# A 12-stage float32 network on one core: the sparse-attention stage rewritten

## The reference

```
hn = rms_norm(h); p = hn @ o_w_in          # q(512) kc vc ks vs kw vw (128 each) gl(24) bg cg hd (512 each)
k_cmp, v_cmp = compress(kc), compress(vc)  # 15 windows of 32 tokens: gelu((window + pos) @ w1) @ w2
o_c = masked_softmax(q . k_cmp / 8) @ v_cmp
o_s = masked_softmax(rope(q) . rope(ks) / 8, causal) @ vs
o_w = masked_softmax(rope(q) . rope(kw) / 8, causal window) @ vw
yc  = gate0 * o_c + gate1 * o_s + gate2 * o_w          # gates = sigmoid(gl), per head and token
yd  = bg * causal_conv3(cg * hd)
h   = h + concat(yc, yd) @ o_w_out
h   = h + moe(rms_norm(h))
```

## Time and profile before

| | us |
|---|---|
| median of 3 runs | 2113.72 |
| the runs | 2109.43, 2113.72, 2114.61 |
| the profiled execution | 2109.94 |
| its span | 2107.9 |
| granted TensorE clock, mean | 0.989 |

### The profile page before, as it was taken

One profiled execution on the slowest core, in us unless ns is written; L12 is line 12 of the kernel. 1 busy time (PEld: TensorE's weight loads), 2 busy tenths in 40 slices (PEclk: granted clock), 3 DMA queues, 4 the chain that ended last, 5 costly groups with the idle time before them and its releaser, 6 DMA issues.

```text
span 2107.9 us, 31941 instructions
## 1 busy us (share of the span) xinstructions
PE 2016.6 (96%) x11820; PEld 1767.6 (84%) x11820; DVE 1577.1 (75%) x2176; ACT 1150.0 (55%) x1687; POOL 394.0 (19%) x192
## 2 busy tenths in 40 slices
PE   7999999999999999999999999999987999999997
PEld 6888987888888889888889998888975888888885
DVE  6777886677777769677778666777785588888887
ACT  5445543554454455554455535445445577777775
POOL 2222003232222310122322432223000300000000
PEclk9999999999999999999999999999998999999999
DMA  8555520455645554355544005555451588888895
GB/s 341 186 194 169 179 90 15 169 197 187 196 167 197 180 187 152 120 179 195 184 170 150 2 15 182 185 194 192 160 180 39 180 331 327 325 327 325 325 329 190
DMA packets 73395, 401.22 MB, mean 190 GB/s; under 512 B 8256, under 2 KB 8384, under 8 KB 41152
## 3 DMA queue, kind: packets, MB, share of 16 engines
q1 hardware_dynamic: 72848, 398.07, 54.1%
q10 hardware_dynamic: 432, 1.57, 0.2%
HBM read 398.57 MB, written 1.05 MB: 190 GB/s over the span
## 4 chain that ended last, share of the span: by engine, by line
PE 76%; DVE 13%; PEld 4%; ACT 3%; issue 2%; POOL 0%; DMA 0%; SPq 0%; ACTq 0%; PEldq 0%; DVEq 0%; POOLq 0%
PE psum L744 18%; PE psum L306 13%; PE psum L307 13%; PE psum L308 13%; PE psum L748 9%; DVE w_lo L290 4%; PE psum L969 2%; PE psum L957 2%; ACT w_hi L283 1%; PE psum L2803 1%; DVE w_lo L296 1%; PE psum L320 1%; PEld psum L306 1%; PEld psum L308 1%; PEld psum L307 1%
## 5 line engine op out<-in xcount | busy, mean ns | idle before, releaser
L290 DVE TENSOR_TENSOR w_lo<-ring,w_hi 128x1024 fp32r<-128x1024 f32 x498 | 742.7, 1521 | 179.4 <-ACT w_hi L283 178.0
L283 ACT ACTIVATE w_hi<-ring 128x1024 fp32r<-128x1024 f32 x744 | 739.9, 1051 | 234.2 <-PEq L500 129.1
L296 POOL TENSOR_TENSOR w_lo<-ring,w_hi 128x1024 fp32r<-128x1024 f32 x132 | 324.0, 2455 | 1079.7 <-ACT w_hi L283 1079.7
L744 PE MATMUL psum<-fT,w_hi 128*128 128x512 f32 x1760 | 422.4, 391 | 12.9 <-DVE w_lo L290 10.5
L744 PEld LDWEIGHTS psum<-fT,w_hi 128*128 128x128 f32 x1760 | 329.6, 188 | 84.3 <-issue 7.6
L306 PE MATMUL psum<-w_hi,hT_hi 128*128 128x384 f32 (+4 forms) x896 | 321.7, 359 | 12.4 <-POOL w_lo L296 4.0
L308 PE MATMUL psum<-w_hi,hT_lo 128*128 128x384 f32 (+4 forms) x896 | 310.7, 347 | 0.0
L307 PE MATMUL psum<-w_lo,hT_hi 128*128 128x384 f32 (+4 forms) x896 | 310.3, 346 | 0.0
L306 PE MATMUL psum<-w_hi,act_hi 128*128 128x512 f32 x616 | 242.4, 394 | 5.5 <-DVE act_lo L842 4.6
L307 PE MATMUL psum<-w_lo,act_hi 128*128 128x512 f32 x616 | 241.2, 392 | 0.0
L308 PE MATMUL psum<-w_hi,act_lo 128*128 128x512 f32 x616 | 239.9, 390 | 0.0
(11 more groups left out here) (485 smaller groups left out, 2413.9 us busy)
## 6 DMA issues: line engine op xcount, KB each, us to landing
ring<-in_stream SPq DMA_DIRECT2D x249, 1024.0 KB, 5.4
ring<-in_stream SPq DMA_DIRECT2D x248, 512.0 KB, 4.3
tables<-in_tables SPq DMA_DIRECT2D x1, 2261.0 KB, 19.9
gain_row<-in_gains ACTq DMA_DIRECT2D x3, 512.0 KB, 3.7
rows<-in_rows SPq DMA_DIRECT2D x1, 1288.0 KB, 22.6
X<-in_x SPq DMA_DIRECT2D x1, 1024.0 KB, 5.0
result<-X SPq DMA_DIRECT2D x2, 512.0 KB, 3.3
columns<-in_columns SPq DMA_DIRECT2D x1, 993.0 KB, 15.0
```

Of the source, the lines that this page charges most:

```text
L283: act.activation(part(w_hi, g, i), ring[:, k, i * PART:(i + 1) * PART], ACT.Copy) \
L290: dve.tensor_tensor(part(w_lo, g, i), ring[:, k, i * PART:(i + 1) * PART], part(w_hi, g, i).bitcast(F32), ALU.subtract) \
L296: pool.tensor_tensor(part(w_lo, g, 2), ring[:, k, 2 * PART:STEP], part(w_hi, g, 2).bitcast(F32), ALU.subtract) \
L744: pe.matmul(psum[:, 4 + 2 * (s % 2) + o, :], w[0][:, o, k, :], fT[:, k, :, :].rearrange("p a c -> p (a c)"), start=k == 0, stop=False, ski ...
```

## The change

The sparse stage keeps its operations but for these:

- The mask is added by PE: `scores_tensor(masked=True)` issues a third matmul with a bf16 identity and a bf16 view of the mask. The maxima are reduced straight from PSUM, and ACT's exps read PSUM with the scale (`masked_max_vector`, `masked_exp_scalar`); a score bank is then marked used by the exps.
- The columns of cg, hd and bg come in another order. cg is multiplied by the square of the row, and hd's copy multiplies by cg, so that the separate product is gone. The row copy stands at step 1.
- The rotations, the windows, the transposes of the rotated q and keys and the scores of group 0 move in among the projections; its maxima and exps too. The transposes of n_tok stand after step 4, the scores after step 5.
- DVE splits the last parts of the compression steps and of the output's first step; POOL does none of them. The output's first step is split before the attention's later groups.
- Products go group by group into both banks of o; the compressed branch comes last.
- The output's first step begins with its convolution half (k = 4 to 7), ahead of and between the transposes of o.
- No `keep_warm` is left in the stage.
- Buffers: half of n_S lies over one parity of w_hi and w_lo; n_zb, n_rope, the squared row and group 0's exps lie in O; other small tiles share space.

```diff
-        def scores_tensor(pe, stage, label, q, k):
+        def scores_tensor(pe, stage, label, q, k, masked=False):
             b = open_bank(pe, label)
-            pe.matmul(b[:, 0:P], q[:, 0:P], k[:, 0:P], start=True, stop=True)
-            pe.matmul(b[:, P:UNIT], q[:, P:SEQ], k, start=True, stop=True).then_inc(*stage.tensor(label))
+            pe.matmul(b[:, 0:P], q[:, 0:P], k[:, 0:P], start=True, stop=not masked, skip_group_check=masked)
+            ins = pe.matmul(b[:, P:UNIT], q[:, P:SEQ], k, start=not masked, stop=not masked, skip_group_check=masked)
+            if masked:
+                ins = pe.matmul(b[:, 0:UNIT].rearrange("p (b c) -> p b c", c=P)[:, 0::2, :], ident_bf16, bias_bf16[:, 0::2, :],
+                                start=False, stop=True, skip_group_check=True)
+            ins.then_inc(*stage.tensor(label))
...
+        def masked_max_vector(dve, stage, name, units, scale, small):
+            for i, u in enumerate(units):
+                dve.wait_ge(*after(f"{u}"))
+                dve.tensor_reduce(small[:, i, :], bank(u)[:, 0:UNIT].rearrange("p (b c) -> p b c", c=P), AX.X, ALU.max).then_inc(*stage.vector())
...
+        def masked_exp_scalar(act, stage, name, units, S, scale, less, sums):
+            act.wait_ge(*after(f"{name} max"))
+            for i, u in enumerate(units):
+                for t, cols in enumerate((slice(0, P), slice(P, UNIT))):
+                    act.activation(S[:, i, cols], bank(u)[:, cols], ACT.Exp, scale=scale, bias=less[:, i, t:t + 1], accum_out=sums[:, i, t:t + 1]) \
+                       .then_inc(*stage.scalar(f"{name} exp"))
+                marks[f"used {u}"] = marks[f"{name} exp"]
...
 PE, sparse_tensor
-            proj_tensor(pe, "sparse", g0, N_KINDS, at, between={2: turn_plain})
+            proj_tensor(pe, "sparse", g0, N_KINDS, at, between={2: turn_plain, 4: turn_rotated, 5: lambda: scores(0)})
-                        keep_warm(pe, b, 0 if which else 11)
+            scores(1)
...
+            turn_units(0)
...
+            scores(2)
...
+            turn_units(1)
+            scores(3)
+            turn_units(2)
...
+            for i in range(3):
+                products(i)
+            turn_units(3)
+            products(3, (0,))
+            finish(0)
+            products(3, (1,))
+            finish(1)
...
+            conv_part(0)
+            turn_tensor(pe, "sparse", sparse, 4, [f"used sparse o {t}" for t in range(TT)], ts=(0,))
+            conv_part(1)
+            turn_tensor(pe, "sparse", sparse, 4, [f"used sparse o {t}" for t in range(TT)], ts=(1,))
+            out_tensor(pe, "sparse", at, 4, begun=((0, 0), (0, 1)))
...
 ACT, sparse_scalar
+            proj_copies_scalar(act, "sparse", at, N_KINDS, n_place, {2: plain}, ahead=True,
+                               later={4: gate, 5: rotated, 7: lambda: exps(0)})
...
+            hidden(0)
+            split_hi(act, c0 + SPARSE_C, c0 + SPARSE_C)
+            hidden(1)
...
+            exps(1)
...
+            turned_units(0)
+            exps(2)
...
+            turned_units(1)
+            exps(3)
+            turned_units(2)
...
+            out_scalar(act, at, "sparse", "used sparse o 1", sparse, 4, ahead=1, turned=turned)
...
 DVE, sparse_vector
+            proj_copies_vector(dve, "sparse", at, N_KINDS, n_place, ahead=True, lasts=range(len(N_KINDS)), row_at=1, scale_of=n_scale,
+                               later={3: lambda: (squared_row(), rotate(0)), 4: lambda: rotate(1), 5: windows, 6: lambda: largest(0)})
+            split_lo(dve, c0 + 1, c0 + 1)
+            split_lo_last(dve, c0 + 1, c0 + 1)
+            weights(0)
+            split_lo(dve, c0 + 2, c0 + 2)
+            split_lo_last(dve, c0 + 2, c0 + 2)
+            tap(0)
+            split_lo(dve, c0 + 3, c0 + 3)
+            split_lo_last(dve, c0 + 3, c0 + 3)
+            largest(1)
...
+            tap(1)
+            weights(1)
+            largest(2)
...
+            tap(2)
+            weights(2)
+            largest(3)
...
+            weights(3)
+            does("sparse conv", dve.tensor_tensor, hT_lo[:, 4:8, :], n_conv[:, :, :], hT_hi[:, 4:8, :].bitcast(F32), ALU.subtract)
+            turn_vector(dve, "sparse", sparse, 4)
+            out_vector(dve, "sparse", at)
...
 POOL
-            split_lo_last(pool, g0, g0)
```

More of the change, by code:

```diff
@@ L524, in proj_tensor @@
                     wait_split(pe, g)
-                for k in range(KT):
+                ks = range(tiles if (s, j) in begun else KT)
+                for k in ks:
                     if isinstance(source, int):
@@ new lines, in scores, with turn_units @@
+            def scores(i):
+                pe.wait_ge(*after("used sparse kt 1"))
+                for u in range(4 * i, 4 * i + 4):
+                    s = u % SLOTS8
+                    scores_tensor(pe, sparse, f"sparse s {u}", n_qr[slot_rows(s), s // 2, :], n_kt[slot_rows(s), u // SLOTS8, :], masked=True)
+            def turn_units(i):
+                for u in range(4 * i, 4 * i + 4):
+                    turn_unit_tensor(pe, sparse, f"sparse pt {u}", n_exps(i)[:, u % 4, :], f"sparse p {i}")
@@ new lines, in products @@
+            def products(i, ts=range(TT)):
+                for u in range(4 * i, 4 * i + 4):
+                    pe.wait_ge(*after(f"used sparse pt {u}"))
+                    br, s = divmod(u, SLOTS8)
+                    for t in ts:
+                        for j, pt in enumerate(unit_blocks(n_unit(u), t)):
+                            v = (VS, VW)[br] + 64 * (s % 2)
+                            pe.matmul(bank(f"sparse o {t}")[:, 64 * s:64 * s + 64], pt, n_tok[:, j, v:v + 64], start=u == 0 and j == 0, stop=False,
+                                      skip_group_check=True)
@@ L1683, in sparse_tensor, with finish @@
+            def finish(t):
+                pe.wait_ge(*after("used sparse vcmp"))
+                pe.wait_ge(*after(f"used sparse pct {t}"))
+                pe.matmul(bank(f"sparse o {t}"), n_pct[:, t, :], n_vcmp.rearrange("p s d -> p (s d)"), start=False, stop=True,
+                          skip_group_check=True).then_inc(*sparse.tensor(f"sparse o {t}"))
+            proj_tensor(pe, "sparse", g0, N_KINDS, at, between={2: turn_plain, 4: turn_rotated, 5: lambda: scores(0)})
             for s in range(SPARSE_C):
@@ L1699, in sparse_tensor @@
                 release(pe, "sparse c", s)
[L1700 to L1706, removed]
-                for i, c0 in enumerate((KS, KW)):
-                    ins = pe.transpose(b[:, i * P:(i + 1) * P], n_tok[:, t, c0:c0 + P], ident)
-                ins.then_inc(*sparse.tensor(f"sparse kt {t}"))
+            scores(1)
             for which in range(2):
@@ L1715, in sparse_tensor @@
                 ins.then_inc(*sparse.tensor(f"sparse hid turned {which}"))
-            pe.wait_ge(*after("used sparse kt 1"))
-            def scores(units):
-                for u in units:
-                    s = u % SLOTS8
-                    scores_tensor(pe, sparse, f"sparse s {u}", n_qr[slot_rows(s), s // 2, :], n_kt[slot_rows(s), u // SLOTS8, :])
-            scores(range(0, 4))
+            turn_units(0)
             pe.wait_ge(*after("used sparse hid turned 1"))
@@ L1788, in sparse_scalar @@
                 split_hi(act, g, g)
[L1789 to L1799 removed]
+            hidden(0)
+            split_hi(act, c0 + SPARSE_C, c0 + SPARSE_C)
+            hidden(1)
+            act.activation(warm[:, :], eps, ACT.Exp)
             for which in range(2):
@@ L1851, in windows @@
                 wait_proj(dve, "sparse", N_KINDS, range(SPARSE_K, SPARSE_K + 2))
-                settle()
+                for which in range(2):
+                    does(None, dve.memset, n_zb[which][:, :, :, CMP_N:], 0.0)
                 for which, pos in enumerate(("pos_k", "pos_v")):
```

240 lines of the change are left out of this document (137 added, 103 removed).

## The result

| | before | after |
|---|---|---|
| median (14 runs each) | 2113.24 us | 2118.85 us |
| range | 2108.14 to 2114.61 | 2113.55 to 2123.64 |
| profiled execution, span | 2109.94, 2107.9 | 2117.55, 2115.6 |

The ratio is 1.0029, 95% interval 1.0021 to 1.0037: 5.6 us slower, where 2102.2 was forecast. In the two traces the sparse stage, from its first projection matmul to the first expert matmul (PE line L2803 before, L2932 after), takes 187.08 us before (1478.18 to 1665.26) and 192.78 after (1480.20 to 1672.98). The 2.0 us by which it starts later in the profile after were lost far ahead of it; subtract them when comparing places. Each kernel has one trace, and its execution need not be a typical one: that of before lies 3.3 us under its median, that of after 1.3.

The account below looks back on a forecast made before the run. DVE was taken to bound 1563 to 1602 us, a serial PE tail 1602 to 1639. Step 1 12.2 us earlier, less 2.5, saves 9.7: forecast 2102.2 us, own range 2099 to 2106, eight in ten 2095 to 2109.

Parts of the forecast that it names:

- the signs by which the prediction said it would be wrong: Compression's first matmul after 1557, output step 1 before 1622 or after 1632, or expert stage length changed by over 2 us.
- the first product: After exps 3 end, near 1597, the first product matmul was to run at clock 0.50.
- no idle before the first channel-major tile: In the projections, moving the row copy to step 1 frees the bank: PE's 2.94 us wait at 1508.36 goes.
- the wait in step 7: In the projections, tile (7, 1) waits for unit 0's exps to free its bank: 1.8 us lost on PE.
- the four PSUM reductions: In attention on DVE, a group's maxima become four reductions straight from PSUM, taking 1.9 us.
- products to step 1: Convolution half, transposes, then ACT's and POOL's work: output step 1 can start 13.2 us after the products.
- the expert stage: Behind the sparse stage, PE-bound: its length stays within 2 us, and a shift passes through to the kernel's end.
- I take 0.13, the nearer row: Score groups on PE: each added mask matmul costs 0.13 us, at most 0.4, so 2.2 us for a group.
- The products themselves pay: 5 us at half clock lose 2.5 us: Products after exps 3: fillers gone, PE's clock starts at half and recovers after 5 us, losing 2.5 us.
- the sum: Start of output step 1: 12.2 us earlier, less 2.5 for half clock in step 1, gives 9.7 us saved.
- the fourth: Products never lift the clock; products, convolution and transposes run at half: 8.8 us slower, 2121 us; chance 0.06.
- Rival 2: More half clock, from the 2.7 us gap before compression, or costlier masks and maxima: saves 4 to 7 us; chance 0.15.

Follow-up runs that it names:

- z1: The changed kernel with only the four mask matmuls of each group issued ahead of its score matmuls, no fillers: 2109.93 us, ratio 0.9985.
- x4: The changed kernel with 51 filler matmuls added ahead of compression, two groups' transposes, the products and output step 1: 2106.22 us, ratio 0.9979.
- y1: x4 with each group's four mask matmuls issued together ahead of its score matmuls: 2101.24 us, ratio 0.9952 against the kernel before.
- z4: y1 with group 0 masked on VectorE and without the 11 fillers ahead of compression: 2096.20 us, ratio 0.9924 against the kernel before.
- x1: The changed kernel with twelve filler matmuls ahead of the first product: 2113.63 us, ratio 1.0009 against the kernel before.
- x3: The kernel before without its 12 fillers ahead of the third group's transposes and 16 ahead of the output: 2112.66 us, ratio 1.0004.

## Why the prediction was wrong

Places in us from the stage's start. "Part 2 ends" is the end of the second token tile's products; the last row is the stage's length.

| | before | forecast | after | z1 | x4 | y1 | z4 |
|---|---|---|---|---|---|---|---|
| compression starts | 76.6 | 76.6 | 80.0 | 76.7 | 80.6 | 80.6 | 74.5 |
| exps 3 end | 123.1 | 118.5 | 128.3 | 119.4 | 123.7 | 120.0 | 115.4 |
| part 2 ends | 145.0 | 135.2 | 149.1 | 142.4 | 142.3 | 138.7 | 134.0 |
| step 1 starts | 160.6 | 148.4 | 162.0 | 155.3 | 155.2 | 151.5 | 146.9 |
| expert matmuls | 187.1 | 177.4 | 192.8 | 186.6 | 183.4 | 178.3 | 175.0 |

Of the signs by which the prediction said it would be wrong, two came. In times of the trace of before, the first compression matmul comes at 1558.2 (80.0 into the stage; the limit was 1557) and step 1 starts at 1640.2 (162.0; the limit was 1632). And the first product, which was to come at clock 0.50, came at 1.00.

Right, by the same steps: no idle before the first channel-major tile; the wait in step 7, 1.8 reckoned, 1.77 found; the four PSUM reductions, 1.9 reckoned and 1.94 found (1.87 in the chain); products to step 1, 13.2 reckoned, 162.0 - 149.1 = 12.9 found, with 3.68 us of idling for 3.7 and a loss of 7.08 - 4.4 = 2.7 in step 1 for 2.5; the expert stage, 442.6 us in both. With both causes mostly gone (y1) the stage takes 178.3 us against the forecast's 177.4; part of that agreement is luck, since step 1 is still 3.1 us late there and the way from it to the expert matmuls 2.2 us shorter than reckoned, without the lost clock in step 1 that the forecast had.

**The step that failed first: "I take 0.13, the nearer row ... the upper end adds 1 us here and 1 us to each later group".** Both ends were prices of the added instruction, 0.13 and 0.4. The cost was in its neighbours: 0.69 a unit, 0.38 of it the overlap of the two units around it. The hint was there: the four units of the earlier trace rows are on row halves in turn and take at most 0.44 us each, and I read that as the price of one unit and not as half that of a pair. Group 0 took 4.1 us for 2.2. Then the clock fell behind the wait in step 7, from 1549 to 1552, for a loss of 1.7 us. So compression started 3.4 us late. Grouping the masks undoes it: 8.9 us alone, 5.0 beside fillers.

**The step that failed second: "The products themselves pay: 5 us at half clock lose 2.5 us".** The clock was at 1.00 when they began, so the gaps ahead of them, which I had counted as the fall, had not lowered it yet; it fell 1.8 us into them and came back only at 1624, in the transposes behind them. The 72 products took 13.93 us for 8.1, 5.8 lost, and the transposes 0.7 more, where the sum had 2.5. And the sum had no half clock for the groups before them, since I counted only idle gaps as causes. The clock fell at about 1576 and 1587 while PE was busy with scores and masks, and the compressed scores took 6.13 us for 3.25. From compression's start to the end of exps 3 the chain needed 48.3 us for 41.9; 43.2 in x4, 39.5 in y1. So there the clock was worth 5.2 us and the parted pairs 3.7, more together than the 6.4 that were lost: the rest of the chain is 2.4 us shorter than I reckoned.

Of the 5.7 us + 9.7 us between forecast and stage (15.4), then: 3.4 by the start of compression, 6.4 from there to exps 3, 4.1 in the products, 0.3 less on the way to step 1, and 1.8 behind it, of which 1.6 in the fillers ahead of the expert matmuls, at half clock after (4.7 us for 14, before 3.1). That last fall was in no term of the sum either. The single removals are worth 12.6 (x4) and 8.9 us (z1), both together 17.6 (y1): they overlap by 3.9. In part that is because a parted pair costs twice as much at half clock: a unit with its mask took 1.07 us at full and 1.91 at half (1577.12 to 1579.03 after).

Of the rivals, the fourth came closest (2121 forecast, 2118.85 measured), at a chance of 0.06, and in part by luck. It has all products and the convolution at half clock; the first products and the whole convolution ran at full. What it charges too much there makes up for what it leaves out, the 9.8 us by which exps 3 end late. Its argument against was that the same products kept 1.00 from 1611 to 1623. There they stood behind fillers and 24 transposes, in x1 and x4 behind fillers, and kept the clock; after, behind 3.6 us in which PE was busy for 0.6, they did not, and once it was down they did not lift it. Rival 2 had the clock fall in the gap before compression: after it fell earlier, behind the wait in step 7, at the same price of 1.7 us; in z1 and z4 it fell behind that very gap.

The Trainium skill (TensorE: Matmul & The Clock Gate, Part 4: PE-mode transpose) was cited for a rule that transposes do not count for the clock. The run x3 disagrees: behind 4.78 us of idling PE did nothing but transposes for 4 us at 0.50, and the clock rose before the 24th. It does not always: in x1 twelve transposes from 1594.05 ran at half from first to last, with scores on both sides.

## What to carry to other kernels

Before putting a matmul between others, ask what these share: if neighbours use different row halves, they run as a pair, and anything of full height between them costs the pair's overlap (0.38 us here, for a mask of 0.14); put it ahead of the whole group. Fillers are worth their place where they fit into a wait (16 ahead of a step of the output: 2.7 us less in its first tile after, about as much before) and cost nothing else. Where they stand behind the wait, on PE's path, reckon both sides: 12 ahead of the products took 2.75 us and gave 5.8; 11 ahead of compression took 2.2 and saved 1.7. When fillers are removed, price every thin stretch behind them at half clock, not only the first microseconds.

## What was not expected of the hardware

- Two float32 units of 64 rows, on different halves, take 0.76 us together and 0.76 us each when alone.
- 64-column float32 products, TensorE busy throughout, did not bring the clock back in 15.6 us (z1, at half from the first to the last), nor in the 12 us that were left of them when it had fallen (after), but kept it at 1.00 for 8.1 us where it stood there (x1, x4).
- The clock fell during busy stretches: 12 us with PE busy for 11.68 were granted 0.70 (1575 to 1587).
- In x3 the clock came back 4.2 us into a run of transposes; behind the products it came back 1.7 us (after) and 3.4 us (z1, when they had just ended) after the first of twelve transposes. In x1 twelve of them between scores did not bring it back. Why it came with transposes and never with the products alone stays open.
